# VectorE centres three tiles and GpSimd five in each inner LayerNorm

## The reference

```python
def _layer_norm(z, g, b, out_dtype):
    z32 = z.astype(jnp.float32)
    mu = jnp.mean(z32, axis=-1, keepdims=True)
    var = jnp.mean(jnp.square(z32 - mu), axis=-1, keepdims=True)
    return ((z32 - mu) * lax.rsqrt(var + LN_EPS) * g + b).astype(out_dtype)

for i in range(DEPTH):
    mods = (jax.nn.silu(c) @ ada_w[i] + ada_b[i]).reshape(bsz, 9, D_MODEL)
    h = _modulate(x, mods, 0)
    y = _swiglu(h, ffn_w_in[i, 0], ffn_w_out[i, 0])
    x = _layer_norm(ALPHA * x + 0.5 * mods[:, 2, None, :] * y, ln_g[i, 0], ln_b[i, 0], dtype)
    h = _modulate(x, mods, 1)
    y = mixer(h)                      # attention for i = 0, HGRN2 for i = 1
    x = _layer_norm(ALPHA * x + mods[:, 5, None, :] * y, ln_g[i, 1], ln_b[i, 1], dtype)
    h = _modulate(x, mods, 2)
    y = _swiglu(h, ffn_w_in[i, 1], ffn_w_out[i, 1])
    x = _layer_norm(ALPHA * x + 0.5 * mods[:, 8, None, :] * y, ln_g[i, 2], ln_b[i, 2], dtype)
```

## Time and profile before

| | |
|---|---|
| median of 3 runs | 2140.7 us (2138.68 to 2141.26) |
| profiled execution, device time | 2141.63 us |
| its span | 2139.9 us, 30931 instructions |
| TensorE busy | 2097.4 us, 98% |
| VectorE, ScalarE, GpSimd busy | 1199.3, 784.7, 246.0 us |
| mean granted TensorE clock | 0.994 of full |
| DMA | 266.34 MB, 41.5% of 16 engines' span |

### The profile page before, as it was taken

One profiled execution on the slowest core, in us unless ns is written; L12 is line 12 of the kernel. 1 busy time (PEld: TensorE's weight loads), 2 busy tenths in 40 slices (PEclk: granted clock), 3 DMA queues, 4 the chain that ended last, 5 costly groups with the idle time before them and its releaser, 6 DMA issues.

```text
span 2139.9 us, 30931 instructions
## 1 busy us (share of the span) xinstructions
PE 2097.4 (98%) x10775; PEld 1720.5 (80%) x10775; DVE 1199.3 (56%) x1878; ACT 784.7 (37%) x1142; POOL 246.0 (11%) x238
## 2 busy tenths in 40 slices
PE   7999999999999999999999999999999999999997
PEld 5788888878888888888888888877878788888886
DVE  6766665655557666654535533467676555333344
ACT  4321222455434222222532222376666545322222
POOL 0000000432113000001300000151121131000002
PEclk9999999999999999999999999999999999999999
DMA  9766752332325657643335632332222123323322
GB/s 319 216 184 196 219 174 72 88 109 80 106 70 186 188 176 226 195 125 101 89 98 164 179 98 76 101 102 77 70 77 69 40 70 99 91 85 113 95 73 84
DMA packets 405669, 266.34 MB, mean 124 GB/s; under 512 B 9416, under 2 KB 366184, under 8 KB 405608
## 3 DMA queue, kind: packets, MB, share of 16 engines
q1 hardware_dynamic: 405608, 265.57, 41.5%
HBM read 263.37 MB, written 2.19 MB: 124 GB/s over the span
## 4 chain that ended last, share of the span: by engine, by line
PE 92%; ACT 3%; DVE 3%; issue 1%; POOL 1%; DMA 0%; SPq 0%; ACTq 0%; POOLq 0%; DVEq 0%
PE ps L1483 26%; PE ps L1485 26%; PE ps L1484 26%; PE ps L1498 1%; PE ps L1499 1%; PE ps L1523 1%; PE ps L1761 1%; PE ps L1504 1%; PE ps L1682 1%; PE ps L1708 1%; PE ps L1529 1%; PE ps L1693 1%; DVE w_lo L837 1%; PE ps L1779 1%; PE ps L1515 1%
## 5 line engine op out<-in xcount | busy, mean ns | idle before, releaser
L837 DVE TENSOR_TENSOR w_lo<-raw,w_hi 128x1024 fp32r<-128x1024 f32 (+2 forms) x384 | 429.1, 1119 | 699.4 <-ACT w_hi L601 699.2
L601 ACT ACTIVATE w_hi<-raw 128x1024 fp32r<-128x1024 f32 (+2 forms) x384 | 371.6, 969 | 1104.9 <-PE ps L1485 1067.2
L1483 PE MATMUL ps<-h_hi,w_hi 128*128 128x512 f32 x1744 | 686.8, 394 | 3.6 <-DVE g L846 2.2
L1485 PE MATMUL ps<-h_hi,w_lo 128*128 128x512 f32 x1744 | 679.4, 390 | 0.0
L1484 PE MATMUL ps<-h_lo,w_hi 128*128 128x512 f32 x1744 | 678.9, 389 | 0.0
L1483 PEld LDWEIGHTS ps<-h_hi,w_hi 128*128 128x128 f32 x1744 | 327.4, 188 | 79.0 <-issue 8.3
L1485 PEld LDWEIGHTS ps<-h_hi,w_lo 128*128 128x128 f32 x1744 | 327.4, 188 | 68.9
L1484 PEld LDWEIGHTS ps<-h_lo,w_hi 128*128 128x128 f32 x1744 | 327.6, 188 | 65.9
L1483 PE MATMUL ps<-g_hi,w_hi 128*128 128x512 f32 x704 | 276.0, 392 | 0.0
L1485 PE MATMUL ps<-g_hi,w_lo 128*128 128x512 f32 x704 | 274.1, 389 | 0.0
L1484 PE MATMUL ps<-g_lo,w_hi 128*128 128x512 f32 x704 | 274.0, 389 | 0.0
(11 more groups left out here) (252 smaller groups left out, 1943.6 us busy)
## 6 DMA issues: line engine op xcount, KB each, us to landing
raw<-in_ffn_w_in_dram SPq DMA_DIRECT2D x176, 512.0 KB, 3.7
ada_raw<-in_ada_w_dram SPq DMA_DIRECT2D x128, 512.0 KB, 4.3
raw<-in_ffn_w_out_dram SPq DMA_DIRECT2D x64, 384.0 KB, 3.4
raw<-in_ffn_w_out_dram SPq DMA_DIRECT2D x64, 320.0 KB, 3.1
raw<-in_hgrn_w_in_dram SPq DMA_DIRECT2D x40, 512.0 KB, 3.7
raw<-in_na_w_qkv_dram SPq DMA_DIRECT2D x24, 512.0 KB, 3.7
boot<-in_ada_w_dram SPq DMA_DIRECT2D x8, 512.0 KB, 6.8
boot<-in_ada_w_dram SPq DMA_DIRECT2D x16, 256.0 KB, 6.1
```

The lines of the kernel that those rows point to most:

```text
L601: nc.scalar.activation(w_hi[s][:, 0:ph.kt, :], raw[s][:, 0:ph.kt, :], ACT.Copy).then_inc(S.w_hi_done, 1)
L837: nc.vector.tensor_tensor(w_lo[s][:, 0:ph.kt, :], raw[s][:, 0:ph.kt, :], w_hi[s][:, 0:ph.kt, :].bitcast(F32), ALU.subtract).then_inc(S.w_l ...
L1483: nc.tensor.matmul(ps[:, bank, :], w_hi[s][:, k, :], a, start=start and k == 0, stop=False)
L1485: ins = nc.tensor.matmul(ps[:, bank, :], w_lo[s][:, k, :], a, start=False, stop=stop and k == ph.kt - 1)
```

## The change

The constant goes from 4 to 3. All that depends on it follows: VectorE centres tiles 0 to 2, GpSimd tiles 3 to 7. The normalise of tile 3 waits for GpSimd's first centring and stands behind the split. In the loop the low part of tile k - 3 follows the normalise of tile k, where it was that of tile k - 4. ScalarE's wait before the copy of the mean and the waits on the counts of both engines are counted with 3 and 5 in place of 4 and 4.

```diff
 NLN = 6
 PIPELINED = ("na", "hg")
-DVE_CENTRED = 4
+DVE_CENTRED = 3
 FIN_ACT = [2, 5, 7]
```

## The result

| | before | changed |
|---|---|---|
| median of 20 executions | 2141.74 us (2138.68 to 2144.06) | 2145.64 us (2142.36 to 2148.09) |
| ratio, 95% interval | | 1.0019 [1.0013, 1.0024] |
| profiled execution | 2141.63 us | 2144.26 us |

The changed kernel is slower by 3.9 us, with an interval of 2.8 to 5.1. The forecast was 1.1 us slower, so the sign was right and the size a quarter of what came. Of the 3.8 us between the forecast time of 2141.8 and the measured one, 1.0 is the starting point: the forecast was added to the median of three executions of the kernel before, 2140.7, and that of its 20 is 2141.74.

What follows compares the result with a forecast made beforehand. TensorE, busy in 98% of the span, was taken as the bound, so edits elsewhere show only where it waits. +0.5 + 0.1 + 0.3 + 0.2 = +1.1 us on a median of 2140.7 gave 2141.8, range 2138.9 to 2145.2.

Steps and rivals of the forecast that it cites:

- LN0, +0.5: LN0 and the attention behind it: GpSimd's bias chain 1.25 us later, less 0.75 slack, costs +0.5 us.
- LN1, LN2 and LN4, +0.4: Splits moved forward, VectorE taken to win the port: +0.1 us for LN1 and LN2 together, +0.3 for LN4.
- (b): GpSimd takes the port in LN1 and LN2, TensorE stalls 1.2 us in each: total +3.5 us, 2144.2; 13%.
- LN3, +0.2: LN3 and HGRN: TensorE gains 0.9 us in the pass but waits again for q_sig; net +0.2 us.
- (a): The LN gains survive, GpSimd's delay doesn't reach TensorE: together -0.9 us, 2139.8; 13%.
- (c): VectorE doesn't get between two GpSimd centrings, so waiting splits wait for the fifth too: +9.9 us, 2150.6; 3%.
- (d): One more stretch of TensorE's clock at the lower level, in LN0 or at 1437, costs up to 1.7 us: 2143.5; 8%.

Runs made afterwards that it cites:

- the repeat: The changed kernel run once more as it is, for a second trace; ratio 1.0020 to the kernel before.
- filled: The changed kernel with nine unused matmuls on TensorE where it waits for q_sig; ratio 1.0017, mean 2144.8 us.
- duties first: The changed kernel, split ahead of GpSimd's fourth centring, mask, first bias and HGRN constants before GpSimd's residuals; ratio 1.0019, 2144.97 us.
- FFN kernel: The kernel before with three tiles on VectorE and five on GpSimd in LN1, LN2 and LN4 alone; ratio 1.0013, median +1.8 us.
- LN3 kernel: The kernel before with three tiles on VectorE and five on GpSimd in LN3 alone; ratio 1.0010, median +1.6 us.
- LN0 kernel: The kernel before with three tiles on VectorE and five on GpSimd in LN0 alone; ratio 1.0001, median +0.3 us.
- split first: The changed kernel, but GpSimd waits for the split of the fourth weight block before its fourth centring; ratio 1.0011, mean 2144.3 us.
- both: The changed kernel with GpSimd waiting for the split before its fourth centring and nine unused matmuls in the q_sig wait; ratio 1.0011, mean 2143.6 us.

## Why the prediction was right or wrong

**LN0, +0.5: right, as far as it can be told.** Changed alone it costs 0.3 us, with an interval of -1.7 to +2.1. The better test is the repeat, whose LN0 began as in the trace of before: the first `h_lo` ran from 415.49 to 416.47 (415.50 to 416.46 foreseen), and TensorE came to L1693 at 446.17 instead of 445.90, 0.3 us later. Its pass is 0.5 to 0.6 us shorter (10.88 to 11.08 us for 11.53; 0.43 was foreseen), and TensorE waits 0.19 to 0.84 us at the first L1693 in all but two of the traces with this LN0 and GpSimd's order unchanged. GpSimd's last residual ended 15.95 to 16.06 us after its first centring (16.05 foreseen). The slack was a little larger than foreseen, since the hand-over took 0.06 us and not 0.18.

**LN1, LN2 and LN4, +0.4: the step that failed.** Measured alone: +1.8. I took two distances from one execution as if they were the kernel's: when TensorE reaches the weights of k = 3 (659.35), and when the split comes after GpSimd's first centring. Then I let 0.01 us decide for VectorE (my own rows give 0.03: 656.60 for the split, 657.86 - 1.29 = 656.57 for the centring). The first made "a few hundredths" of what is 0.26 to 1.16 us of waiting where TensorE comes earlier and the split doesn't meet the fourth centring; these are 3.4 of the 6.0 us in the table above. The second is not one number either. Over the traces with three tiles on VectorE, where no added wait held the split or kept the fourth centring from it:

| split starts after the first centring | it takes | where |
|---|---|---|
| 2.79 us (2 times) | 2.10 | filled and duties first, LN2 |
| 3.21 to 3.29 (4) | 1.61 to 1.68 | duties first LN1, LN3; repeat LN3; FFN kernel LN4 |
| 3.44 to 3.53 (3) | 1.35 to 1.45 | filled LN3, repeat LN2, FFN kernel LN1 |
| 3.61 to 3.72 (6) | 1.22 to 1.26 | changed LN1 to LN3, repeat LN1, LN4, filled LN4 |
| 3.78 to 3.79 (4) | 2.33 to 2.36 | changed LN4, FFN kernel LN2, filled LN1, LN3 kernel |

The first rows all end at the same place: 2.79 + 2.10, 3.21 + 1.68 and 3.53 + 1.35 are 4.88 to 4.89, and that is 1.22 after 3.67. A split issued earlier than 3.67 waits for the third centring. (In the duties-first kernel the fourth was held back by its added wait, which doesn't touch that.) The latest free one came at 3.72, and from 3.78 on it waits for the fourth. The free window is some 0.1 us wide, and the place that the prediction computed, 656.60 or 3.79 us after the first centring, lies just behind it. Where the split falls depends on TensorE: with the spread at the upper clock level VectorE's normalise of tile 0 starts 0.45 us before GpSimd's first centring, at the lower mostly 0.2 to 0.55 us after it. LN0 had the first in the trace of before and LN1 the second; I laid each out from its rows and did not ask whether a LayerNorm keeps its state. So the tie that I gave to VectorE goes to GpSimd in all four cases in which it arose as I computed it, and the other splits escape it by arriving earlier, not by winning. Rival (b), named for LN1 and LN2 with 13% and +3.5 us, was the right mechanism. It struck in at most one LayerNorm of each trace with the order open, and once in each of LN1 to LN4.

**LN3, +0.2: the mechanism right, the size short.** Measured alone: +1.6. The sum for GpSimd held: the last residual ended 17.9 to 18.2 us after the first centring wherever LN3 had three tiles and GpSimd's order (18.3 foreseen; 18.2 before, and 17.5 in the FFN kernel, whose split in LN3 came ahead of the residual and took 1.28 us). The scan starts 23.75 to 24.4 after it (24.0 before, 23.3 in the FFN kernel), and TensorE goes on from `q_sig` 9.8 us after the scan (10.1 with duties first). So TensorE's next start hangs on GpSimd's first centring, and what the pass gains is a longer wait: 2.66 us for "near 2.5". The first wait for `h_hi` in it was 0.25 to 0.75 us for "near 0.8" (1.38 in the LN3 kernel, whose split met the fourth centring). The gain itself depends on the execution: with four tiles the pass took 11.7 to 12.6 us (4 traces) and with three 11.2 to 12.8 (8), so the 0.9 was read off one of the longer ones. Counted from the first centring TensorE goes on at `q_sig` at 33.6 to 34.2 us with three tiles; with four it is 33.8 in before and the LN0 kernel, where a residual had held the split, and 33.0 to 33.1 in the other two. The change costs nothing here against the first kind and 0.5 to 1.1 us against the second, and the prediction had the first. From the first weights of the pass to `q_sig` it is 30.3 to 31.3 with four (4 traces) and 30.8 to 32.3 with three (8), a mean of +0.7, but the first weights come anywhere from 1.6 to 2.8 us after the first centring in these, so how much of it is the change is not settled. The clock behind the wait comes on top with 0.7 to 0.8.

**Rivals.** (a) fell: what the passes gained in LN0 and LN3 was given back. (b) holds, worth 1.3 us. (c) fell: with the centrings back to back and the next one free to go, a waiting split went in ahead of it in all six cases. (d), which I gave 8%, is seen at `q_sig` and worth an estimated 0.7 to 0.8 us.

**The sum.** Of 4.1 us in the means, 1.3 go with the order at the port and 0.7 with the clock at `q_sig`, and the kernel with both cured still loses 2.1 ± 0.4. The granted clock that stands on record for every execution shows of what kind the rest is. A span times the share not granted is the clock time lost in it (to 2.1 us for one execution, since the clock has three decimals, but means over many tell more); what is left of the time is the rest. Means in us:

| kernel | clock time lost | the rest, less that of before |
|---|---|---|
| before | 12.8 ± 0.2 | |
| change, with its repeat | 14.2 ± 0.4 | +2.6 ± 0.3 |
| LN0 alone | 13.4 ± 0.9 | 0.0 ± 0.6 |
| LN1, LN2, LN4 | 12.3 ± 0.8 | +2.7 ± 0.6 |
| LN3 alone | 14.0 ± 0.7 | +0.7 ± 0.3 |
| split first | 14.4 ± 0.5 | +1.1 ± 0.7 |
| wait filled | 12.9 ± 1.1 | +3.2 ± 0.6 |
| both | 13.2 ± 0.5 | +1.5 ± 0.4 |

So some 1.5 us of the change are clock time and 2.6 are other time. Most of the latter lies in LN1, LN2 and LN4, and ordering the port halves it. The clock time is largest where LN3 has three tiles and lower in the two kernels whose wait at `q_sig` is filled, though each of these differences is no more than two or three times its error. LN0's spread ran partly at the lower level in 5 of 8 traces with three tiles in LN0 and in none of 4 with four, which looks like 1.6 us more, but the kernel with only LN0 changed lost 0.3 us, and that with both cured has only 0.5 ± 0.5 more clock time than before. What the 1.5 us of other time are that both cures leave stays open: in that kernel's trace the three passes took 43.6 us, as before, and the way to `q_sig` in LN3 is 0.5 us longer. One trace doesn't tell what the other ten had.

**The range** missed by 0.4 us at its upper end, 2145.2, for two reasons. (b) and (d) were priced as alternatives, and they add to each other and to the forecast: 1.1 + 1.3 + 0.7 = 3.1 us. And it stood on 2140.7, the median of three executions, which is 1.0 us below that of twenty. With 2141.74 under it the same range would have held 2145.64, without its terms being any better.

## What to carry to other kernels

Where a step is moved next to a shared resource, lay it out against the phase of the other engines in several executions or LayerNorms, not in one: here 0.1 us of arrival decided between 1.22 and 2.34 us, the phase moved by a whole microsecond with TensorE's clock, and a step that had slack in one trace was waited for by up to 1.2 us in another. An engine's wait that grows because the work ahead of it got faster is not free if the engine is the bound: TensorE's clock can fall behind it, so price the wait itself. And add up rivals that can happen together before setting a range.

## What the runs showed of the hardware

**The port's boundary.** The split, with two SBUF inputs, went in at the first boundary between GpSimd's centrings each time it stood waiting, and GpSimd's next instruction, where no added wait held it, took 2.26 to 2.29 us and not 1.30. Blocking was complete, never a slowing: 2.29 to 2.36 us is 1.22 and the rest of the other's instruction. The Trainium skill, SBUF — State Buffer, section "Who interferes with whom", says that issue order decides and that the other fully blocks. The traces agree for a split 0.01 to 0.04 us behind the start of a centring (4 cases), and add that a waiting split is not passed by the next instruction of a row. Behind a residual the stamps don't decide: the split 0.06 us behind in the earlier trace rows went first, that 0.08 us behind in the LN0 kernel waited.

**One form that was passed.** The `p_neg` of 128x4 numbers stood 4.78 us through seven GpSimd instructions back to back, while `h_lo` and splits got in at the next boundary. It has one SBUF input, as have `f_sig` and `zt`, which took 0.92 and 0.88 us beside residuals. The same section names `tensor_scalar` among the forms that can take the shared pair, and says nothing of a difference in who gets in. That they meet, three instructions show here; that one is passed, a single one, and the same instruction for the other head went through in 0.17 us at 435.49, inside such a row. I would not build on either.

**The clock.** At `q_sig` a wait of TensorE of 1.44 us or less came with no stretch at the lower level in any of nine traces, one of 2.5 us and more with one in three of five. And the same code in LN0 ran its spread in 4.69 us at 2.4 GHz in one execution and in 6.30 in another, partly at 1.2 GHz (mean granted clock 0.73), which alone is 1.6 us, 40% of the effect that was to be measured.
